# First feed-forward layer of a two-block model: partition sums of the modulation vectors by transposes and row sums

## What is computed

```python
def adaln(cvec, w, b):
    m = jax.nn.silu(cvec) @ w + b
    return jnp.split(m[:, None, :], N_MOD, axis=-1)

def ffn(h, wg, wu, wd):
    return (jax.nn.silu(h @ wg) * (h @ wu)) @ wd

x = x + ga2 * ffn(modulate(rms_norm(x, norm_ffn[i]), sh2, sc2), w_gate[i], w_up[i], w_down[i])
```

## Time and profile before

| | us |
|---|---|
| median of 3 runs | 3532.85 |
| lowest, highest | 3523.05, 3534.52 |
| profiled execution | 3535.11 |
| its span, first to last instruction | 3533.0 |
| TensorE busy | 3429.5 (97%) |
| VectorE busy | 2315.2 (66%) |
| ScalarE busy | 563.9 (16%) |
| GpSimd busy | 162.2 (5%) |

### The profile page before, as it was taken

One profiled execution on the slowest core, in us unless ns is written; L12 is line 12 of the kernel. 1 busy time (PEld: TensorE's weight loads), 2 busy tenths in 40 slices (PEclk: granted clock), 3 DMA queues, 4 the chain that ended last, 5 costly groups with the idle time before them and its releaser, 6 DMA issues. The chain is left out here.

```text
span 3533.0 us, 58173 instructions
## 1 busy us (share of the span) xinstructions
PE 3429.5 (97%) x24909; PEld 2769.2 (78%) x24909; DVE 2315.2 (66%) x4391; ACT 563.9 (16%) x1072; POOL 162.2 (5%) x168
## 2 busy tenths in 40 slices
PE   7999999999999999999999999999999999999999
PEld 4456666677878888889998766867877888888888
DVE  2277887775468988898777555555654756644644
ACT  2232222221010000000003133232221000000000
POOL 1000000000000000000001000000001000000000
PEclk9998999999899999999999999999999999999999
DMA  9833443345678787866674634545224666654443
GB/s 338 264 80 101 117 117 107 101 124 150 201 247 267 246 253 258 261 217 213 202 237 158 214 123 139 167 143 164 99 96 146 223 215 217 212 182 155 176 167 131
DMA packets 663409, 638.46 MB, mean 181 GB/s; under 512 B 43490, under 2 KB 630752, under 8 KB 662128
## 3 DMA queue, kind: packets, MB, share of 16 engines
q1 hardware_dynamic: 554464, 563.16, 49.8%
q10 hardware_dynamic: 108016, 71.44, 7.0%
q0 software_dynamic: 672, 0.15, 0.0%
HBM read 628.41 MB, written 6.29 MB: 180 GB/s over the span
## 5 line engine op out<-in xcount | busy, mean ns | idle before, releaser
L1998 PE MATMUL bank<-work,extra 128*128 128x256 f32 x2112 | 463.0, 379 | 0.0
L664 DVE SCALAR_TENSOR_TENSOR work<-weight_ring,silu_c,work 128x256 f32<-128x256 f32 x1050 | 450.6, 502 | 0.0
L1998 PEld LDWEIGHTS bank<-work,extra 128*128 128x128 f32 x2112 | 400.7, 190 | 54.1
L1998 PE MATMUL bank<-weight_ring,work 128*128 128x256 f32 x1408 | 318.2, 385 | 8.4 <-ACT work L2131 7.6
L2199 DVE TENSOR_TENSOR work<-weight_ring 128x2048 f32<-128x2048 f32 (+2 forms) x72 | 129.7, 1801 | 296.8 <-DMA weight_ring<-in_w_gate_up 160.7
L1998 PEld LDWEIGHTS bank<-weight_ring,work 128*128 128x128 f32 x1408 | 269.5, 193 | 46.2 <-issue 8.3
L1011 PE MATMUL bank<-work,x_channels 128*128 128x256 f32 (+1 forms) x704 | 231.7, 478 | 0.0
L2745 PE MATMUL bank<-work,weight_ring 128*128 128x512 f32 x448 | 205.4, 604 | 0.9 <-PEq L2441 0.9
L1011 PEld LDWEIGHTS bank<-work,x_channels 128*128 128x128 f32 x704 | 131.5, 192 | 75.4 <-issue 63.8
L1998 PE MATMUL bank<-weight_ring,extra 128*128 128x256 f32 x704 | 159.3, 379 | 2.0 <-DVE extra L2194 2.0
L1998 PE MATMUL bank<-work 128*128 128x256 f32 x704 | 159.2, 379 | 0.0
(11 more groups left out here) (462 smaller groups left out, 5474.5 us busy)
## 6 DMA issues: line engine op xcount, KB each, us to landing
weight_ring<-in_w_mod SPq DMA_DIRECT2D x80, 2048.0 KB, 10.0
weight_ring<-in_w_gate_up SPq DMA_DIRECT2D x44, 2048.0 KB, 9.4
weight_ring<-in_w_in SPq DMA_DIRECT2D x26, 2048.0 KB, 9.3
weight_ring<-in_w_gate SPq DMA_DIRECT2D x22, 2048.0 KB, 8.3
weight_ring<-in_w_up SPq DMA_DIRECT2D x22, 2048.0 KB, 13.9
weight_ring<-in_w_down SPq DMA_DIRECT2D x20, 2048.0 KB, 8.1
weight_ring<-in_w_mod ACTq DMA_DIRECT2D x32, 1024.0 KB, 5.4
weight_ring<-in_w_out SPq DMA_DIRECT2D x16, 2048.0 KB, 10.2
```

The source lines that it names most:

```text
L664: ins = v_.scalar_tensor_tensor(a, w[:, k, :], c, a, ALU.mult, ALU.add)
L1998: last = mm(product(u, p), right[p][:, k, :], left[p][:, k, :], start=k == 0, stop=k == 7)
```

## The change

The products with ones become transposes of the same tiles into bank 7, 128 columns each. VectorE sums each of them along its row into a new small tile `mod_raw`, and adds the bias from there. The semaphores and who waits for them stay as they were, but for VectorE's wait for its own sum.

```diff
@@ -1971,7 +1971,10 @@
                 v = mods[i][2]
-                mod_sums(nc, st, sums[:, j % 2, 0:v, :], v, 0, S["mod_columns"])
+                for n in range(2 * v):
+                    w, t = n // 2, n % 2
+                    last = nc.tensor.transpose(st.psum[7][:, n * P:(n + 1) * P], sums[:, j % 2, w, t * P:(t + 1) * P], st.c("ident"))
+                last.then_inc(S["mod_columns"], 1)
 
@@ -2227,9 +2230,11 @@
-                x = st.psum[7][:, 0:4].rearrange("p (t v) -> p t v", v=2)
+                x = st.psum[7][:, 0:2 * v * P].rearrange("p (n a) -> p n a", n=2 * v)
+                raw = st.mod_raw[:, 0:2 * v]
+                vl(nc.vector.tensor_reduce(raw, x, AX.X, ALU.add))
                 for w in range(v):
-                    last = tt(st.mod[of][:, w, 2 * c:2 * c + 2], x[:, :, w], b_mod[of][:, 2 * c:2 * c + 2], ALU.add)
+                    last = tt(st.mod[of][:, w, 2 * c:2 * c + 2], raw[:, 2 * w:2 * w + 2], b_mod[of][:, 2 * c:2 * c + 2], ALU.add)
                     if w < v - 1:
                         vl.mark(last)
                 last.then_inc(S["mod_kept"], 1)
@@ -3276,6 +3281,7 @@
         st.eps = sb("eps", [P, 4])
+        st.mod_raw = sb("mod_raw", [P, 4])
         st.sink = sb("sink", [P, NH2])
```

## The result

| | before | change |
|---|---|---|
| median of 7 runs each, us | 3530.23 | 3543.32 |
| lowest, highest | 3520.33, 3534.52 | 3538.55, 3550.81 |
| profiled execution | 3535.11 | 3545.50 |
| from the stage's first product to that of in2 | 862.74 | 873.20 |
| TensorE busy | 3429.5 | 3423.0 |

The ratio of the times is 1.0043, with a 95% interval of 1.0029 to 1.0057. The change makes the kernel slower, by 10 to 20 us; the medians lie 13.1 us apart. The two profiled executions lie 10.4 us apart, and the stage accounts for it: it takes 10.5 us longer. Behind it the programs take 1630.0 and 1630.7 us.

What follows compares the result with a forecast made beforehand. VectorE's loop with its transfers was taken to bound the stage, with 2.5 us of slack in the up half behind a busier TensorE. Terms 3.1 + 2.5 + 2.3 - 0.7 = +7.2 us on 3532.85 gave 3540 us, range 3528 to 3550.

Steps and rivals of the forecast that it cites:

- What bounds the kernel: First feed-forward stage: TensorE is busiest, but VectorE's loop with its weight transfers, 2.5 us short of TensorE's pace, decides.
- TensorE's price: TensorE's 90 transposes for 180 records, 0.11 us each: 9.9 us less, two steps 49.9 us.
- the rival of the whole record: On TensorE, each transpose costs its whole 273 ns; two steps 50.9 us, about +8 us, 3541; chance 0.02.
- VectorE's price: VectorE's 29 new row sums: 0.70 us for four tiles, 0.43 for two, 16.8 us in all.
- The rival of a dearer sum: VectorE's sum behind post_up (L2235) costs 1.14 us instead of 0.70: +7.0 us, 3547; chance 0.14.
- Term 1: Up half, steps 2 to 17: one four-tile sum in each of VectorE's eight loop turns, +3.1 us.
- The slack of the whole up half is thus 2.5 us: Up half: eight undisturbed VectorE turns would end at 1495.2 but ended at 1497.65, TensorE being slower by then.
- Term 2: Steps 18 to 21, VectorE without waits: three four-tile sums and one two-tile sum reach TensorE's wait whole, +2.5 us.
- Terms 3 and 4: Down half: sums delay the second part's weight sums, +2.3 us; last down step, TensorE keeps two groups' gain, -0.7 us.
- TensorE's gain: VectorE's loop has room, so TensorE's relief counts: at best the whole 9.9 us, 3523; chance 0.07.
- They cancel: Up-half transfers shorten to 13.7 us, 4 us less over eight turns, the rest is covered: 3533 to 3536; chance 0.18.
- The moved tile: mod_raw shifts the weight ring by 32 bytes and lengthens transfers: 3545, or 3547 by the splitting rule; chance 0.05.

Runs made afterwards that it cites:

- transposes alone: The change without VectorE's row sum, partition sums left out (bias added to each transposed tile's first column), against the kernel before: 3526.68 us, ratio 0.9995.
- the sum alone: The kernel before, products with ones kept, plus VectorE's row sum of bank 7 into an unread tile: 3536.84 us, ratio 1.0032 against before.
- the fastest kernel: The change with row sums and the up half's first two modulation multiplications per vector (L661) moved to ScalarE: 3518.38 us, ratio 0.9968 against before.
- the kernel before with the first blocks on ScalarE: The kernel before, each vector's first two up-half modulation multiplications (L661) moved from VectorE to ScalarE: 3525.15 us, ratio 0.9990 against before.
- the change with the tile at the end: The change with mod_raw allocated last, so ring, work and extra keep their old places: 3540.16 us, ratio 1.0032 against the kernel before.
- the sums on ScalarE: The change with row sums made in place in bank 7 by ScalarE's accumulation, VectorE only adding the bias: 3529.0 us, ratio 0.9993 against before.
- partial sums on GpSimd in the kernel before: The kernel before with VectorE's 45 additions of two partial sums (L672) moved to GpSimd: 3605.61 us, ratio 1.0216 against before.

## Why the prediction was right or wrong

The direction and the main mechanism were right, and the measured median of 3543.3 lies in the range (3528 to 3550). The size was too small: 7.2 us were forecast, and the medians lie 13.1 apart, the profiled stages 10.5. The likeliest time, 3540, is nearer to the median than that, because the kernel before came out 2.6 us lower in seven runs than in the three that I counted from. The measurement can tell the loss from none; a loss of over 0.3% I gave 0.25. One term failed in size, and one cost was left out, the clock.

**What bounds the kernel** held: TensorE busy without a gap, and yet VectorE's loop decides. The transposes alone (0.9995) and the sum alone (1.0032) show both halves of it.

**TensorE's price.** Forecast 49.9 us for two steps, measured 49.88. 0.11 us for a transpose was right, and the rival of the whole record is out: it wanted 50.9. The Trainium skill (TensorE: Matmul & The Clock Gate, Part 4: PE-mode transpose) gives about 275 ns for a transpose. The records have that duration here (273 ns), but it is not what one costs in a row of them.

**VectorE's price.** 0.70 and 0.43 taken from the copy and the maximum, measured 0.68 and 0.42. The rival of a dearer sum is out.

**Term 1, the failed step: "The slack of the whole up half is thus 2.5 us".** Forecast +3.1, measured +5.5. I measured transfers from the issue of the up weights and multiplied the first turn's 35.40 us by eight. SyncE's queue in the kernel before, the gate issues of the first and of the eighth turn (the up issues are in the earlier trace rows):

```profile
1133.55 0.37 SPq L349 DMA_DIRECT2D weight_ring<-in_w_gate  x1
...
1482.19 0.37 SPq L349 DMA_DIRECT2D weight_ring<-in_w_gate  x1
```

and, of the change, both issues of the eighth:

```profile
1486.80 0.37 SPq L349 DMA_DIRECT2D weight_ring<-in_w_gate  x1
1487.26 1.52 SPq L349 DMA_DIRECT2D weight_ring<-in_w_up  x1
```

In the first turn of before the up issue (1134.01) follows the gate issue by 0.46 us, as in the change. In the eighth of before it follows by 1.30 (1482.19, and 1483.49): TensorE, the slower there, frees the up slot later. That looked like a loop already stretched by TensorE. But the later issue does not make the up weights land later. In the eighth turn of the fastest kernel (first blocks and sums on ScalarE) it follows by 3.45 us, and VectorE has the weights 14.18 us behind the gate issue, as early as in the turns with 0.46. Measured from the gate issue, which in these two kernels VectorE alone releases, the loop is:

| | before | change |
|---|---|---|
| weight sums of the even step to gate issue, every turn | 34.93 to 34.94 | 35.67 to 35.68 |
| the eight, together | 279.5 | 285.4 |
| gate issue to the next even step's sums, eight together | 119.6 | 119.1 |
| eight turns | 399.0 | 404.5 |

VectorE's part is the same to 0.01 us in all eight turns of before, also in those where I believed TensorE to be the slower. There was no slack at all: 1098.61 + 279.5 + 119.6 = 1497.7, which is the measured start, and from there on the prediction rightly had VectorE as the bound up to TensorE's wait at 1605.30. The other traces bear it out. VectorE's part of the eight turns is 279.5 us in each of the four kernels without the sum and with the first blocks on VectorE, and 285.4 or 285.5 in the three with one sum; the rest is 118.8 to 120.8 in these seven, and does not go with the sum. Where TensorE does hold the loop up, the measure shows it: in the kernel before with the first blocks on ScalarE, VectorE's part goes from 33.88 us up to 35.24. So the sum counts from the first turn: 8 x 0.74 = 5.9 us, less 0.5 from the rest of the turns. With a slack of zero the forecast would have been 8 x 0.70 = 5.6 in this term and 9.7 in all, against 10.5 measured in the stage.

**Term 2**, forecast +2.5, measured +2.7. **Terms 3 and 4**, forecast +2.3 and -0.7, together +1.6, measured +2.2. That they agree is partly luck. The prediction called the clock "no part of the question", which held for before and not for the change: the 1.5 us of the last fall are in the 2.2, and without them some 0.7 or less would be left (an estimate from the two rows at 1848.14 and 1849.65). The last sum was hidden as forecast: in the change VectorE still waits 0.38 us for ScalarE's root, where it waited 0.83:

```profile
1907.24 0.42 DVE L2235 TENSOR_REDUCE mod_raw<-bank 128x2 f32<-128x256 f32 x1
...
1908.73 1.75 DVE L2406 RECIPROCAL work<-work 128x256 f32<-128x256 f32 x1 [0.38 <-ACT work L2171]
```

**The other rivals.** TensorE's gain did not count, but it is real: it shows (6.8 us) as soon as VectorE has room. "They cancel" is out; the transfers did not become shorter. The moved tile is out (1.0004).

What stays open: the three kernels with the sum on VectorE stand at ratios of 1.0043, 1.0032 and 1.0032, with stages of 873.2, 873.9 and 875.4 us. The stage explains 10 to 13 us and the ratios 7 to 20; whether the change itself loses more than its sum alone can't be told from these intervals. The share of the clock is open too: the change with the tile at the end has the same waits, but a fall behind only two of its four longest, and the longer stage.

## What to carry to other kernels

A loop through a queue that works in order is measured from its first issue, the one that the suspected engine releases: a later issue behind it may be late and cost nothing. Where the engine's own part is the same to the hundredth in every turn, nothing else has been pacing it. If its loop also ends in a wait of the others, as here, its slack is zero, however busy another engine looks.

Taking work from the engine with the highest busy share is worth nothing while a loop of another engine with transfers is as long; shorten that loop first, then the relief pays. The edit as it stands, with the sum left on VectorE, lengthens the loop again and showed no gain even then. Here ScalarE was the place with room: with the sums and the first blocks there, the kernel takes 0.9968 of the time of before and is the fastest of all that ran.

A wait that an edit brings to TensorE is not priced by its own length alone: look at the granted clock behind it.

Taking work off an engine should be priced by the time from one start to the next behind it: a neighbour's toll may move to the next instruction.

## What the runs showed of the hardware

**Most transfers have one of two lengths.** From the gate issue to VectorE's first sum of the up weights (4 MB have landed by then) it mostly takes 14.1 to 14.6 us or 15.3 to 16.1. The transfers by queue, around one of each kind, in the kernel before (1133.5 to 1148) and in the change (1486.8 to 1502.5). An issue has its KB and the us to its landing; a queue its packets, MB and share of the engines' time:

```profile
weight_ring<-in_w_gate SPq DMA_DIRECT2D x1, 2048.0 KB, 8.0
weight_ring<-in_w_up SPq DMA_DIRECT2D x1, 2048.0 KB, 13.6
```

```profile
q8 instruction: 1, 0.02, 0.5%
weight_ring<-in_w_gate SPq DMA_DIRECT2D x1, 2048.0 KB, 8.2
weight_ring<-in_w_up SPq DMA_DIRECT2D x1, 2048.0 KB, 15.1
```

The eleven traces without additions on GpSimd have 88 such turns. In 40 of them a packet of a queue named "instruction", 0.93 to 2.11 us long, starts in the first 13 us behind the gate issue: 37 took 15.26 to 16.09 us and three, with the packet close to the issue, 14.33 to 14.91. In 38 there is none of over 0.2 us: 34 took 14.13 to 14.57, but four took 14.94 to 15.70, among them the fourth turn of before (15.15 us from the gate issue at 1281.28). So the packets go with some 1.2 us more, and they are not the only thing that lengthens a transfer. This is a coincidence in time, not an experiment.

**TensorE's clock falls behind waits of a few us.** In the up and down halves of the same eleven traces, from the second step on, 19 of the 23 waits of 2.63 to 5.12 us were followed by the lower clock, and one (of 1.91 us) of the 19 waits of 1.04 to 2.52 us. What decides among waits of the same length these traces do not show: 2.86 us with the sums on ScalarE left the next group at 5.62 us, 2.83 us in the change made it 7.26.

**GpSimd's two-input addition hardly advances beside VectorE's.** It takes 0.72 us alone, and two take 9.85 us beside VectorE's sums of 2048 (partial sums on GpSimd in the kernel before). In the other direction, as the places of the rows suggest, GpSimd's product of 1.3 us takes about 1 us from VectorE's multiplications (four L661 2.16 us instead of 1.13, or the 28 behind them 12.18 instead of 11.16).

**Row sums from PSUM.** VectorE sums 128x512 in groups of 128 in 0.68 us, as fast as it copies 128x512 (0.69); ScalarE with its accumulator needs 0.27 and 0.19 us for each 128x128, and starts them 0.28 us apart.
